# Three edits to a decoder block kernel: modulation products between two weight slabs, parameter tables and the saved input reordered on a DMA queue, one wait step shorter in a scan

## The reference

```
mod = silu(c) @ w_ada + b_ada            # 9 vectors of 1024: shifts, scales, gates
h = modulate(rms_norm(x, g_ffn1), sh1, sc1)
x = x + 0.5 * gt1 * ((silu(h @ w1_a) * (h @ w3_a)) @ w2_a)      # D_FF = 2816
h = modulate(rms_norm(x, g_mix), sh2, sc2)
x = x + gt2 * hybrid_mixer(h)            # w_in, short conv, S5 state space, gates, w_out
h = modulate(rms_norm(x, g_ffn2), sh3, sc3)
x = x + 0.5 * gt3 * ((silu(h @ w1_b) * (h @ w3_b)) @ w2_b)
out = rms_norm(x, g_final)
```

## Time and profile before

| what | value |
|---|---|
| median of 3 runs | 2392.77 us |
| the profiled execution's own time | 2392.29 us |
| its span in the trace | 2389.7 us |
| TensorE matmul busy | 2308.2 us (97%) |
| VectorE busy | 909.8 us (38%) |
| ScalarE busy | 320.6 us (13%) |
| GpSimd busy | 1100.9 us (46%) |
| TensorE's share of the chain that ended last | 93% |
| mean granted clock of TensorE | 0.983 |
| data moved | 194.29 MB, mean 81 GB/s |

### The profile page before, as it was taken

One profiled execution on the slowest core, in us unless ns is written; L12 is line 12 of the kernel. 1 busy time (PEld: TensorE's weight loads), 2 busy tenths in 40 slices (PEclk: granted clock), 3 DMA queues, 4 the chain that ended last, 5 costly groups with the idle time before them and its releaser, 6 DMA issues.

```text
span 2389.7 us, 27721 instructions
## 1 busy us (share of the span) xinstructions
PE 2308.2 (97%) x10370; PEld 1898.9 (79%) x10370; DVE 909.8 (38%) x1219; ACT 320.6 (13%) x372; POOL 1100.9 (46%) x824
## 2 busy tenths in 40 slices
PE   5899999999999899999999989999999999999997
PEld 4788788878888678888888867887888888888886
DVE  6645124331012699475665544436011101110134
ACT  3311000000011331010101121115110001000112
POOL 3354444444445453444444455543544444444452
PEclk8999999999999999999999999999999999999998
DMA  7344124321121332223222144411111111111111
GB/s 282 106 147 133 44 85 117 114 79 47 50 47 50 115 97 75 84 80 88 84 75 88 53 167 132 137 47 36 53 49 48 48 49 47 50 46 51 41 39 70
DMA packets 258446, 194.29 MB, mean 81 GB/s; under 512 B 21524, under 2 KB 238752, under 8 KB 257248
## 3 DMA queue, kind: packets, MB, share of 16 engines
q1 hardware_dynamic: 234752, 154.52, 21.3%
q10 hardware_dynamic: 23648, 39.20, 5.2%
HBM read 167.34 MB, written 25.17 MB: 81 GB/s over the span
## 4 chain that ended last, share of the span: by engine, by line
PE 93%; DVE 3%; ACT 1%; SPq 1%; issue 0%; DMA 0%; POOL 0%; DVEq 0%; POOLq 0%; ACTq 0%
PE unit_a L486 32%; PE unit_b L486 31%; PE unit_c L486 12%; PE unit_d L486 12%; PE unit_d L726 1%; PE unit_a L565 1%; SPq L340 1%; PE unit_b L565 1%; DVE xr L1105 1%; PE unit_c L609 1%; DVE rstd L1062 1%; PE unit_c L711 1%; PE unit_d L701 1%; PE unit_d L724 1%; PE unit_c L522 0%
## 5 line engine op out<-in xcount | busy, mean ns | idle before, releaser
L456 POOL TENSOR_TENSOR w_high<-raw,ones 128x512 fp32r<-128x512 f32 x408 | 545.3, 1336 | 1220.1 <-PE unit_b L486 395.7
L458 POOL TENSOR_TENSOR w_low<-raw,w_high 128x512 fp32r<-128x512 f32 x408 | 555.8, 1362 | 32.0
L486 PE MATMUL unit_a<-h_high,w_high 128*128 128x512 f32 x1072 | 333.7, 393 | 6.0 <-POOL w_low L458 4.7
L486 PE MATMUL unit_a<-h_low,w_high 128*128 128x512 f32 x1072 | 331.2, 390 | 0.0
L486 PE MATMUL unit_a<-h_high,w_low 128*128 128x512 f32 x1072 | 331.0, 390 | 0.0
L486 PE MATMUL unit_b<-h_high,w_high 128*128 128x512 f32 x1072 | 330.5, 389 | 0.0
L486 PE MATMUL unit_b<-h_high,w_low 128*128 128x512 f32 x1072 | 330.1, 389 | 0.0
L486 PE MATMUL unit_b<-h_low,w_high 128*128 128x512 f32 x1072 | 330.0, 389 | 0.0
L1153 DVE TENSOR_TENSOR s<-s,unit_b 128x1024 f32<-128x1024 f32 x44 | 53.7, 1221 | 655.5 <-PE unit_b L486 652.9
L486 PEld LDWEIGHTS unit_a<-h_high,w_high 128*128 128x128 f32 x1072 | 200.6, 189 | 48.4 <-POOL w_low L458 5.1
L486 PEld LDWEIGHTS unit_a<-h_low,w_high 128*128 128x128 f32 x1072 | 202.0, 188 | 42.5
(11 more groups left out here) (233 smaller groups left out, 2266.0 us busy)
## 6 DMA issues: line engine op xcount, KB each, us to landing
raw<-in_w_a SPq DMA_DIRECT2D x60, 512.0 KB, 4.1
raw<-in_w_b SPq DMA_DIRECT2D x60, 512.0 KB, 3.8
raw<-in_w_in SPq DMA_DIRECT2D x44, 512.0 KB, 3.9
ada_raw<-in_w_ada SPq DMA_DIRECT2D x8, 2048.0 KB, 7.9
ada_raw<-in_w_ada SPq DMA_DIRECT2D x8, 1536.0 KB, 7.0
ada_first<-in_w_ada SPq DMA_DIRECT2D x8, 1024.0 KB, 14.2
sg_kept<-s ACTq DMA_DIRECT2D x16, 512.0 KB, 2.6
s<-sg_kept ACTq DMA_DIRECT2D x16, 512.0 KB, 3.3
```

Source lines behind the costliest of these rows:

```text
L456: pool.tensor_tensor(high, raw[:, r, rows, :], one, ALU.mult).then_inc(high_split, 1)
L458: pool.tensor_tensor(w_low[:, r % 2, rows, :], raw[:, r, rows, :], high.bitcast(F32), ALU.subtract).then_inc(slab_split, 1)
L486: last = pe.matmul(unit[u][:, t], w, x[:, k, t], start=(k == 0 and part == 0), stop=(k == kts - 1 and part == 2))
```

## The change

There are three edits in the order of work, and one in addresses.

1. In `up` of TensorE, in every hardware loop turn of the two chunks that carry modulation work, the small products come between slab A and slab B where they came behind slab B. In DVE the bias addition comes right behind the weighted sum and ahead of the multiplication with `unit_b`. The unrolled first turn keeps its order on TensorE.
2. On SP, the six parameter DMAs go from the third chunk to the place between the second and the third slab load of `u`, behind a wait for `x_final`; the store of `x_kept` goes there too, behind the parameter DMAs.
3. In the scan the first instruction of a level waits as the others do, for all but the last.
4. The tables lie 4 KB lower in SBUF, and `tmp` lies above them.

```
-        lam = sb("lam", [P, 2, KP], rM + 56 * KB)
...
+        lam = sb("lam", [P, 2, KP], rM + 52 * KB)
...
-                    if name == "ffn1" and n == 2:
-                        sp.wait_ge(slab_used, here)
-                        load_parameters()
...
             for r in range(NT):
+                if r == 2:
+                    sp.wait_ge(x_final, 2 * KD)
+                    load_parameters()
+                    sp.dma_start(x_kept, x_res[:, :, :].rearrange("p k t -> p (k t)")).then_inc(x_kept_done, 16)
                 load(at["u"].slab + r, r, w_in[:, :, 24 + r, :])
-            sp.wait_ge(x_final, 2 * KD)
-            sp.dma_start(x_kept, x_res[:, :, :].rearrange("p k t -> p (k t)")).then_inc(x_kept_done, 16)
...
                     slab(here.slab + 2 * i, 0, A_, here.unit[A_] + i, h_high, h_low, KD)
-                    slab(here.slab + 2 * i + 1, 1, B_, here.unit[B_] + i, h_high, h_low, KD)
                 if with_ada and n < 2:
                     pe.wait_ge(ada_summed, 8 * n + i + 2)
                     take(C_, here.unit[C_] + i)
                     ada_tiles(ada_sum, 4 - n, C_)
+                if not isinstance(i, int):
+                    slab(here.slab + 2 * i + 1, 1, B_, here.unit[B_] + i, h_high, h_low, KD)
...
                         ada_columns(ada_sum, ada_raw, many * P)
+                        cols = slice(first, first + 8 * many)
+                        dve.wait_ge(ada_full, 8 * n + i + 3)
+                        dve.tensor_tensor(
+                            mod[:, cols].rearrange("p (i t) -> p i t", t=many)[:, i, :], unit[C_][:, 0:many],
...
+                            add).then_inc(unit_free[C_], 1)
                     dve.wait_ge(unit_free[A_], here.unit[A_] + i + 1)
...
-                    if with_ada:
-                        cols = slice(first, first + 8 * many)
-                        dve.wait_ge(ada_full, 8 * n + i + 3)
...
                                 if n >= 2:
-                                    level_start = to == from_ == 0 and kk == 2 * pair
-                                    dve.wait_ge(scan_step, 4 * 4 * LEVELS * t + n - (0 if level_start else 1))
+                                    dve.wait_ge(scan_step, 4 * 4 * LEVELS * t + n - 1)
```

More of the change, by code:

```diff
@@ L219, in block_kernel @@
         ada_sum = small("ada_sum", [P, 4 * P])
-        lam = sb("lam", [P, 2, KP], rM + 56 * KB)
[L222 to L226, removed]
+        lam = sb("lam", [P, 2, KP], rM + 52 * KB)
+        dt_ = sb("dt_", [P, KP], rM + 52 * KB + 128)
+        q = [sb(f"q{n}", [P, KP], rM + 52 * KB + 192 + 64 * n) for n in range(8)]
+        b_in = sb("b_in", [P, 2, KP, H], rM + 53 * KB)
+        pv = sb("pv", [P, 2, J, KP], rM + 55 * KB)
+        tmp = sb("tmp", [P, 2, 4 * 9 * H], rM + 59 * KB)
         pw = sb("pw", [P, 2, 9, KP], rA + 9 * KB)
@@ L348, in load @@
                 sp.dma_start(raw[:, r, 0:tiles_k, :], src).then_inc(slab_loaded[r], 16)
[L350 to L362, removed]
             def ffn(name, w1, w3, w2, with_ada):
@@ L400, in _, with load_parameters, as_states @@
             w_in = a["w_in"][0].rearrange("(k p) (m n) -> p k m n", p=P, n=P)
+            def load_parameters():
+                def as_states(ap):
+                    return ap.rearrange("(k g) p -> (g p) k", g=2)
+                with nc.allow_non_contiguous_dma(reason="small parameter tables"):
+                    sp.dma_start(lam[:, 0, :], as_states(a["a_re"][0])).then_inc(lam_loaded, 16)
+                    sp.dma_start(lam[:, 1, :], as_states(a["a_im"][0])).then_inc(lam_loaded, 16)
+                    for g2 in range(2):
+                        per = a["log_dt"][0].rearrange("(k g) -> g k", g=2)[g2:g2 + 1, :]
+                        sp.dma_start(dt_[NS * g2:NS * g2 + NS, :], per.to_broadcast([NS, KP])).then_inc(lam_loaded, 16)
+                    for part, b in enumerate(("b_re", "b_im")):
+                        sp.dma_start(b_in[:, part, :, :], a[b][0].rearrange("(k g) p h -> (g p) k h", g=2)).then_inc(b_loaded, 16)
             for r in range(NT):
+                if r == 2:
+                    sp.wait_ge(x_final, 2 * KD)
+                    load_parameters()
+                    sp.dma_start(x_kept, x_res[:, :, :].rearrange("p k t -> p (k t)")).then_inc(x_kept_done, 16)
                 load(at["u"].slab + r, r, w_in[:, :, 24 + r, :])
-            sp.wait_ge(x_final, 2 * KD)
-            sp.dma_start(x_kept, x_res[:, :, :].rearrange("p k t -> p (k t)")).then_inc(x_kept_done, 16)
             n = 0
@@ L1150, in up @@
                         ada_columns(ada_sum, ada_raw, many * P)
+                        cols = slice(first, first + 8 * many)
+                        dve.wait_ge(ada_full, 8 * n + i + 3)
+                        dve.tensor_tensor(
+                            mod[:, cols].rearrange("p (i t) -> p i t", t=many)[:, i, :], unit[C_][:, 0:many],
+                            vt[:, B_ADA + first:B_ADA + first + 8 * many].rearrange("p (i t) -> p i t", t=many)[:, i, :],
+                            add).then_inc(unit_free[C_], 1)
                     dve.wait_ge(unit_free[A_], here.unit[A_] + i + 1)
```

## The result

The changed kernel takes 2455.79 us, the median of 4 runs (2453.57 to 2458.58), beside 2393.32 us for the kernel before (4 runs, 2392.29 to 2394.54). The ratio is 1.0263, with a 95% interval of 1.025 to 1.0276: 62.5 us slower. Slower was forecast, but 2421 us with a range up to 2434. The profiled execution took 2458.1 us, with a span of 2455.5 us, 65.8 more than the span before.

A forecast was written before the change was run, and what follows sets the result against it. The prediction took TensorE, 97% busy, to bound the kernel. Gain at `down`, waits, slow restarts and late slab 2 summed as -10.6 + 20.7 + 6 + 13 = +29.1 on 2392.29, forecast 2421 us, range 2402 to 2434.

The forecast's parts named there:

- Edits 3 and 4: Mixer scan and SBUF addresses: shorter scan waits help DVE only where it has slack, 0 with 1 us either way; addresses 0.
- the sum's last instruction: Chunk 0, weighted sum on DVE: its last instruction falls behind POOL's start and costs 1.0 to 1.3 us more.
- Slow restarts: TensorE after seven new waits of 2.1 to 2.5 us: restarts at half rate, bounds 0 and 11.9, taken as +6 us.
- The waits: Chunks 0 and 1: TensorE waits for the weighted sum after slab A, 14.4 + 2.1 + 4.2 = +20.7 us.
- The gain at `down`: Ends of chunks 0 and 1: `down` starts when slab B ends, without a slow first slab, together -10.6 us.
- Edit 2: Stage `u`: table loads hold SP 25.0 us, then the store; TensorE starts slab 2 10 to 16 us late, taken as +13.
- short waits: Chunks 0 and 1: POOL does not hold the sum, waits are 1.2 and 0.3 us, clock stays up; +13, 2405; chance 0.22.
- ready in time: Middle of each turn: DVE ends the sum by slab A's end, no waits; 2382 to 2395 us; chances 0.04 faster, 0.05 unchanged.
- nothing of edit 2 shows: Stage `u`: slab 2 comes in time while the waits for the sum stay; +16, 2408 us; chance 0.05.

The follow-up runs named there:

- mods_only: The kernel before with only the first edit (small products between slabs A and B, earlier bias addition): 2413.05 us, ratio 1.008.
- scan_back: The changed kernel with the scan's old full waits put back: 2426.15 us, ratio 1.0138 to the kernel before.
- mods_mid_slab: The kernel before with the small modulation products inside slab B, ahead of its sixth row tile, bias addition ahead of DVE's multiplication: 2382.43 us, ratio 0.9956.
- scan_two_levels: The kernel before, with the scan's full wait kept only at every other level: 2394.2 us, ratio 1.0003.
- dma_only: The kernel before with only the moved parameter loads and `x_kept` store, and the new addresses: 2409.53 us, ratio 1.0069.
- tables_ahead: The kernel before with the parameter loads ahead of slab 2 of `u` and the `x_kept` store behind all four slab loads: 2390.86 us, ratio 0.9993.
- mid_and_copy: The kernel before with small products in the middle of slab B and ACT copying the first two `u` results before its sines: 2388.89 us, ratio 0.9983.

## Why the prediction was right or wrong

**The step that failed** is "Edits 3 and 4": "The scan lies beside slabs of the mixer; no wait of TensorE for it is among the waits", and so "0, with 1 us either way". What was priced was DVE's time. What mattered was POOL's: it was let in at the full waits or 1.0 us behind them, and without them it was kept out until the scan ended, so that TensorE waited 11.6 and 11.5 us for its slabs. That cost 32.2 us alone and 29.6 within the change. No rival had it, and the prediction had used the very lock for the sum's last instruction. The trace had shown it, too: eight rows of 3.15 to 3.30 us among rows of 1.14 in one scan, each with a POOL row begun just before, four at a level start and four one row behind it. (The waits changed are 52, not 56: the first level of a scan has none.)

**Second, a term too small.** Slow restarts: I took half of seven. Five of the seven waits of chunk 0 brought one (six in mods_only and in scan_back), at 1.6 us each (12.64 - 11.03), 8 us instead of 6. The small products behind a wait also took 1.05 instead of 0.75 us. These two are the 4 us by which chunk 0 is over its forecast.

**Right, by its own numbers.** The waits: 2.17 in turn 1 (2.1 forecast), about 2.4 in turns 2 to 7, the sum at X + 13.1. In chunk 1 a turn grew from 22.46 to 23.05 us, 0.59 (0.6 forecast), of which only 0.33 is listed as waiting. The gain at `down`: confirmed by mods_mid_slab, -11.4 for -10.6 (0.75 and 0.15 make 0.90 there, not 0.94; the 3.4 stays). Edit 2: +11.7 for +13, with the tables and then the store ahead of the slab as reasoned; TensorE stood for 16.2 us, where I wrote some 18. The Trainium skill ("DMA: Bandwidth & Descriptors", "Two DMAs through the same engine are not ordered") allows the later load to pass. This one did not: its issue began at 868.29 and it reached POOL 16.6 us later. One case says nothing against a rule that only promises no order. The rivals "short waits", "ready in time" and "nothing of edit 2 shows" are ruled out by the wait rows.

**In the unchanged stages:** 2.3 us ahead of the first small products and 2.1 in the last stage. Both differ between traces of kernels that change nothing there: the first small products start anywhere from 87.50 (the kernel before, the earliest of all) to 89.81, at 89.22 in scan_two_levels for one, and the last stage takes 930.9 us in scan_two_levels and 933.0 in dma_only. In the longer kind its last small products run at a granted clock of 0.50 (2437.2 to 2442.0 in the kernel after) for 0.98 before. Why it fell there, and what moves the start, stays open.

## What to carry to other kernels

A wait that costs its own engine nothing can be the gap on which another engine lives. Before removing one, look for the other user of the port: rows of it that begin at that wait or up to 1 us behind it, and rows of this engine that are too long there (3.15 us for 1.14). One gap is enough, but there must be one within the time that the waiting engine is ahead.

Put small work not at the next boundary but where its input is ready: half a slab later, and the same edit turned from +20.7 to -11.4 us. Of DMAs that are moved ahead of a needed load, add up the delays and hold the sum against the time that the load has: the small ones held the queue 24 us and cost nothing by themselves, the store behind them then cost some 17.

## What the hardware showed

- A POOL instruction of 1.29 us waits as long as DVE's stream of scan instructions has no gap: 26.36 us for what was left of 112 of them. A gap of some 0.1 us (one full wait in place of all but the last) lets it in, and its next instruction follows at once; it is also let in 1.0 us behind such a gap (917.46), and in a loop's turn without one in the rows (1085.28).
- A wait of TensorE of 2.2 to 2.5 us brought a slow restart in 17 turns of 21 (the kernel after, mods_only, scan_back); 1.6 us each. One of 3.23 us, ahead of slab 2 of `u` in tables_ahead, brought none. After 11.5 us it cost 3.0, ahead of small products (3.5 us, mid_and_copy) 7.8.
- Six table loads of 4-byte or 64-byte pieces hold the issuing queue for 24 to 25 us; most of it, 16.9, shows on the last one.
